# Modulation of a two-layer block gathered in one accumulator a layer, and the mixing steps in another order

## The reference

```python
c_act = jax.nn.silu(c)
for l in range(2):
    mod = c_act @ ada_w[l] + ada_b[l]        # 1024 -> 6144
    shift1, scale1, gate1, shift2, scale2, gate2 = split(mod, 6)
    h = rms_norm(x, norm1_g[l]) * (1 + scale1) + shift1
    z = h @ w_in[l]
    ...                                       # differential attention -> y_attn
    u = silu(layer_norm(causal_conv31(ga * sigmoid(gb)), conv_ln_g, conv_ln_b))
    y_conv = u @ w_conv_o[l]
    x = x + (1 + gate1) * ((g_attn * y_attn + g_conv * y_conv) @ w_out[l])
    h2 = rms_norm(x, norm2_g[l]) * (1 + scale2) + shift2
    f_gate, f_up = split(h2 @ w_ffn_in[l], 2)
    x = x + (1 + gate2) * ((silu(f_gate) * f_up) @ w_ffn_out[l])
out = rms_norm(x, final_g)
```

## Time and profile before

| | |
|---|---|
| median of the timed runs | 1102.91 us |
| the profiled execution's own time | 1105.96 us |
| its span | 1104.1 us |
| TensorE busy | 1079.3 us (98%) |
| VectorE busy | 821.9 us (74%) |
| ScalarE busy | 525.1 us (48%) |
| bytes read | 227 MB, mean 207 GB/s |
| VectorE, pieces | 84 of 1281 ns and 12 of 749 ns, 116.6 us |
| TensorE, group sums (L503) | 192 rows, 22.2 us |
| mean granted TensorE clock | 0.994 of full |

### The profile page before, as it was taken

How to read it: one execution, slowest core, us unless ns; L and a number is a source line. 1 busy time by engine, 2 the same in 40 slices (tenths; PEclk the granted TensorE clock), 3 DMA queues, 4 the chain that set the end, 5 groups by cost and what they waited for, 6 DMA issues and landing times.

```text
span 1104.1 us, 19435 instructions
## 1 busy us (share of the span) xinstructions
PE 1079.3 (98%) x8322; PEld 1028.9 (93%) x8322; DVE 821.9 (74%) x1096; ACT 525.1 (48%) x613; POOL 30.3 (3%) x54
## 2 busy tenths in 40 slices
PE   6999999999999999999999999999999999999998
PEld 5888799999998989979999999999898899999998
DVE  6878589887775899957887787869999576555552
ACT  4455665554434535545543433454455455344441
POOL 5100000000000010000000000000000000000000
PEclk9999999999999999999999999999999999999998
DMA  8666248888893554328698989846442375655551
GB/s 239 188 229 243 95 172 297 276 286 283 308 330 109 179 175 153 115 77 269 197 315 271 354 305 315 306 151 231 159 153 77 125 250 160 201 180 191 172 172 39
DMA packets 132845, 230.38 MB, mean 209 GB/s; under 512 B 6569, under 2 KB 60183, under 8 KB 132761
## 3 DMA queue, kind: packets, MB, share of 16 engines
q1 hardware_dynamic: 130404, 227.04, 61.3%
q0 software_dynamic: 1440, 0.85, 0.5%
q10 hardware_dynamic: 917, 1.27, 0.3%
HBM read 227.29 MB, written 1.06 MB: 207 GB/s over the span
## 4 chain that ended last, share of the span: by engine, by line
PE 71%; DVE 18%; ACT 6%; issue 3%; DMA 1%; SPq 0%; POOL 0%; DVEq 0%; POOLq 0%; ACTq 0%
PE mm L430 64%; DVE lo L1245 6%; DVE cacc L1335 5%; ACT hi L833 3%; PE mm L473 2%; PE pv L503 2%; ACT pB L912 1%; DVE ada_acc L1266 1%; DVE sB L1343 1%; DVE qk L1358 1%; PE pa L541 1%; DVE hf L1356 1%; DVE qk L1357 1%; DMA swap<-qk 1%; DMA xin<-in_x_dram 1%
## 5 line engine op out<-in xcount | busy, mean ns | idle before, releaser
L430 PE MATMUL mm<-act_hi,hi 128*128 128x256 f32 x1760 | 493.6, 284 | 2.5 <-ACT act_hi L901 1.8
L430 PE MATMUL mm<-act_hi,lo 128*128 128x256 f32 x1760 | 487.3, 280 | 0.0
L430 PE MATMUL mm<-act_lo,hi 128*128 128x256 f32 x1760 | 469.6, 280 | 0.0
L1245 DVE TENSOR_TENSOR lo<-raw,hi 128x2048 fp32r<-128x2048 f32 (+1 forms) x159 | 359.6, 2265 | 131.5 <-ACT hi L833 129.5
L833 ACT ACTIVATE hi<-raw 128x2048 fp32r<-128x2048 f32 (+1 forms) x160 | 302.1, 1892 | 232.0 <-PE mm L430 184.4
L430 PEld LDWEIGHTS mm<-act_hi,hi 128*128 128x128 f32 x1760 | 332.9, 189 | 6.4 <-issue 4.9
L430 PEld LDWEIGHTS mm<-act_hi,lo 128*128 128x128 f32 x1760 | 332.9, 189 | 0.4
L430 PEld LDWEIGHTS mm<-act_lo,hi 128*128 128x128 f32 x1760 | 322.2, 189 | 0.0
L430 PE MATMUL mm<-u_hi,hi 128*128 128x256 f32 x608 | 170.8, 281 | 0.0
L430 PE MATMUL mm<-u_lo,hi 128*128 128x256 f32 x608 | 169.8, 279 | 0.0
L430 PE MATMUL mm<-u_hi,lo 128*128 128x256 f32 x608 | 169.6, 279 | 0.0
(11 more groups left out here) (263 smaller groups left out, 950.3 us busy)
## 6 DMA issues: line engine op xcount, KB each, us to landing
ada_raw<-in_ada_w_dram SPq DMA_DIRECT2D x96, 512.0 KB, 5.7
raw<-in_w_ffn_in_dram SPq DMA_DIRECT2D x88, 512.0 KB, 5.4
raw<-in_w_in_dram SPq DMA_DIRECT2D x40, 1024.0 KB, 5.2
raw<-in_w_ffn_out_dram SPq DMA_DIRECT2D x20, 1024.0 KB, 6.2
raw<-in_w_up_dram SPq DMA_DIRECT2D x16, 1024.0 KB, 6.8
raw<-in_w_down_dram SPq DMA_DIRECT2D x16, 1024.0 KB, 7.7
raw<-in_w_out_dram SPq DMA_DIRECT2D x12, 1024.0 KB, 5.5
raw<-in_w_in_dram SPq DMA_DIRECT2D x16, 512.0 KB, 6.1
```

The costliest lines, as they stand in the source:

```text
L430: ins = pe.matmul(o, w[:, kk, fs], a[:, k, :], start=(k == 0 and i == 0 and f % 2 == 0), stop=(ends and i == len(pairs) - 1), skip_group_c ...
L1245: v(dve.tensor_tensor(lo[:, c % RING, 0:nk, :], raw[:, c % RING, 0:nk, :], hi[:, c % RING, 0:nk, :].bitcast(F32), ALU.subtract), "lo_done")
```

## The change

A piece is now 16 **contiguous rows** of `ada_w` (all 6144 columns, 384 KB). Partition 8k+b holds columns b\*768 to b\*768+767 of row k, 3072 bytes that lie together in memory. Each layer has 64 such pieces and one accumulator of 128 x 768, in a ring of four. silu(c) must then stand eight times over, each value on eight partitions: GpSimd spreads it (`c_wide`) and TensorE turns it. The sum over the 16 rows goes against an 8-column selector (`blocks`), so that one matmul gives eight column tiles: six matmuls a layer instead of 48. All of them stand at the norm ahead of the layer, none between chunks: layer 0's before the first block's last norm, layer 1's three within `sum_squares_late` and three behind it. VectorE adds the bias once a layer, ahead of `gain1`. Pieces: 10, 54 and 64 in the three stages. `keep_warm` has four matmuls more ahead of `up` and two more ahead of each FFN.

Beside that, in the mixing `heads_out(1, (1, 2))` comes ahead of the second sum, ScalarE's `heads_rstd(3)` and VectorE's `heads_normed(3)` come before the squares and their sum, and at the start lambda's matmul and its copy come one chunk earlier.

```diff
-ADA_W = D
-ADA_T = ADA_W // P
-ADA_GROUPS = MODS // ADA_T
-ADA_RING = 3
-ADA_ACCS = 2
-ADA_P = KD
+ADA_B = 8
+ADA_K = P // ADA_B
+ADA_T = MODS // ADA_B
+ADA_W = ADA_T * P
+ADA_RING = 4
+ADA_P = D // ADA_K
...
+    c[i, C_BLK + i % ADA_B] = 1.0
...
-    stages = [(range(first[("in", 2)] + 2, first[("out", 1)] + 1), 1, lambda c: 2.0 if c - first[("in", 2)] in (4, 6) else 1.0),
+    stages = [(range(first[("in", 2)] + 2, first[("out", 1)] + 1), 10, lambda c: 2.0 if c - first[("in", 2)] in (4, 6) else 1.0),
...
-                    src = t["ada_w_2"][i // ADA_GROUPS, k * P:(k + 1) * P, i % ADA_GROUPS * ADA_W:(i % ADA_GROUPS + 1) * ADA_W]
+                    src = t["ada_w_2"][l, k * ADA_K:(k + 1) * ADA_K, :].rearrange("k (b f) -> (k b) f", b=ADA_B)
...
-                if c in ada_at:
-                    ada_sums(c, ada_at)
...
+            def ada_sums(l, tiles):
+
+                if tiles[0] == 0:
+                    pe.wait_ge(sem("ada_used"), (l + 1) * ADA_P)
+                b = bank(2) if tiles[0] == 0 else pv[2]
+                for f in tiles:
+                    ins = pe.matmul(b[:, f:MODS:ADA_T], ada_acc[:, l, f * P:(f + 1) * P], blocks, start=(f == 0), stop=True, skip_group_check=True)
+                if tiles[-1] == ADA_T - 1:
+                    full(ins, 2)
...
+            wait("c_rows_ready")
+            full(pe.transpose(b[:, P + NMOD:P + NMOD + ADA_P], c_wide[0:ADA_P, :], ident[0:ADA_P, 0:ADA_P]), 0)
...
-            chunk(("in", 1), 1, act_hi, act_lo)
             wait("lam_ready")
             full(pe.matmul(bank(2)[:, 0:LAYERS], ones[0:1, :], lams[0:1, 8:8 + LAYERS], start=True, stop=True), 2)
+            chunk(("in", 1), 1, act_hi, act_lo)
...
-            ada_sums(first[("up", 0)], ada_between)
-            keep_warm(WARM + 0)
+            keep_warm(WARM + 4)
...
-                    ada_sums(first[(0, "in", 3)], ada_between)
+                    ada_sums(0, range(ADA_T))
...
-                heads_out(1, (1,))
+                heads_out(1, (1, 2))
                 sum_of("csq_added", hf[:, 0, :], 1)
-                heads_out(1, (2,))
...
-                ada_sums(first[(l, "ffn", 0)], ada_between)
-                keep_warm(2)
+                keep_warm()
...
-                    sum_squares_late()
-                    ada_sums(first[(1, "in", 3)], ada_between)
+                    sum_squares_late(between=lambda: ada_sums(1, range(0, ADA_T // 2)))
+                    ada_sums(1, range(ADA_T // 2, ADA_T))
                     keep_warm(2)
...
+                log_tables()
+                heads_rstd(3, full("a")[:, 0:S], "banka_free")
                 wait("centred")
                 a(act.activation(csq[:, :, :], cacc[:, :, :], ACT.Square), "csq_ready")
-                heads_rstd(3, full("a")[:, 0:S], "banka_free")
...
+            pool.dma_start(c_rows[0:ADA_P, :], t["c_2"][0].rearrange("(r p) -> r p", p=ADA_K)).then_inc(sem("c_rows_loaded"), 16)
...
+                ada_columns(l)
```

More of the change, by code:

```diff
@@ L68 @@
 C_ID, C_ONE = 0, P
-C_FREQ, C_ADD, C_UP = 2 * P, 2 * P + 1, 5 * P + 1
-C_ALL = 8 * P + 1
+C_FREQ, C_BLK = 2 * P, 2 * P + 1
+C_ADD = C_BLK + ADA_B
+C_UP = C_ADD + 3 * P
+C_ALL = C_UP + 3 * P
 def constants():
@@ L177, in two_blocks @@
     first = {name: ids[0] for name, (_, ids) in groups.items()}
[L178 to L185 removed]
+    pieces = LAYERS * ADA_P
+    stages = [(range(first[("in", 2)] + 2, first[("out", 1)] + 1), 10, lambda c: 2.0 if c - first[("in", 2)] in (4, 6) else 1.0),
+              (range(groups[("out", 0)][1][1], first[(0, "in", 3)]), ADA_P - 10, lambda c: 0.85 if c < first[("down", 0)] else 1.3),
+              (range(first[(0, "ffn", 0)], first[(1, "in", 3)]), ADA_P, lambda c: 1.0 if c < first[(0, "down", 0)] else 0.9)]
+    ada_pos = []
     for window, count, share in stages:
         until = np.cumsum([share(c) for c in window[:-2]])
[L188 to L192 removed]
+        for j in range(count):
+            ada_pos.append(window[int(np.searchsorted(until, (j + 0.5) / count * until[-1]))])
     pack, srcs = {}, [
         ("g_mix_pre", t["g_mix_pre"][0], KD), ("g_mlstm", t["g_mlstm_out"][0], MH), ("g_mix_post", t["g_mix_post"][0], KD),
[L199 removed]
+        ("g_mlp_pre", t["g_mlp_pre"][0], KD), ("g_mlp_post", t["g_mlp_post"][0], KD),
         ("final", t["final_g_2"], KD)]
@@ L246, in two_blocks @@
         ada_raw = sb("ada_raw", [P, ADA_RING, ADA_W])
[L247 removed]
+        ada_acc = sb("ada_acc", [P, LAYERS, ADA_W])
         cst = sb("cst", [P, C_ALL])
@@ L289, in two_blocks @@
         adab = sb("adab", [P, P], on=start)
+        c_rows = sb("c_rows", [P, ADA_K], on=start)
+        c_wide = sb("c_wide", [P, P], on=start)
         cwr = sb("cwr", [P, LAYERS, GF], on=start)
@@ L490, in chunk @@
                 ins.then_inc(sem("mm_done"), 1)
-                if c in ada_at:
-                    ada_sums(c, ada_at)
-            def ada_sums(c, where, part=None):
-                l, q, count = where[c]
-                for a in range(count) if part is None else (part,):
-                    i = l * ADA_GROUPS + q + a
-                    pe.wait_ge(sem("ada_used"), (i + 1) * ADA_P)
-                    b = bank(2) if a == 0 else pv[2]
-                    for f in range(ADA_T):
-                        to = a * ADA_T + f
-                        ins = pe.matmul(b[:, to:to + 1], ada_acc[:, i % ADA_ACCS, f * P:(f + 1) * P], ones[:, 0:1], start=(to == 0), stop=True,
-                                        skip_group_check=True)
-                    if a == count - 1:
-                        full(ins, 2)
+            def ada_sums(l, tiles):
[6 more added lines that the diff above has]
+                    full(ins, 2)
             def product(name, *acts, **kw):
@@ L534, in sums_of_added, with sum_squares_late @@
                 n("sq_ready", 2)
-            def sum_squares_late(last=((6,), (7,))):
+            def sum_squares_late(last=((6,), (7,)), between=None):
                 for tiles in ((4, 5),) + last:
+                    if between and tiles == last[0]:
+                        between()
                     wait("sq_ready")
@@ L601, in _ @@
             pe.transpose(b[:, 0:NROW], rows[0:NROW, :], ident[0:NROW, 0:NROW])
-            full(pe.transpose(b[:, P:P + NMOD], adab[0:NMOD, :], ident[0:NMOD, 0:NMOD]), 0)
+            pe.transpose(b[:, P:P + NMOD], adab[0:NMOD, :], ident[0:NMOD, 0:NMOD])
+            wait("c_rows_ready")
+            full(pe.transpose(b[:, P + NMOD:P + NMOD + ADA_P], c_wide[0:ADA_P, :], ident[0:ADA_P, 0:ADA_P]), 0)
             bank("a")
@@ L1457, in _ @@
             advance(groups[("in", 1)][1][0])
+            link(dve.tensor_copy(nlam[:], full(2)[:, 0:LAYERS]), "bank2_free")
             wait("tables_ready")
@@ L1460, in _ @@
             advance(groups[("in", 1)][1][1])
-            link(dve.tensor_copy(nlam[:], full(2)[:, 0:LAYERS]), "bank2_free")
             rope(qk1, swap1, 0, "k")
```

52 lines of the change are left out of this document (18 added, 34 removed).

## The result

The changed kernel takes 1095.68 us (median of 4 runs, 1094.22 to 1096.14), the kernel before 1103.13 (4 runs beside it): ratio 0.9927, 95% interval 0.9914 to 0.9939. It is faster by 7.45 us. The forecast was 1089.5 with a range of 1085.5 to 1095.0: right in sign, short of the size by half, and outside the range by 0.7.

The account below looks back on a forecast made before the run. TensorE, busy 98% of the span, was taken as the bound, with VectorE and ScalarE as slow in layer 0's FFN. Terms summed to 14.5 us off the profiled 1105.96, giving 1091.5; the median forecast was 1089.5, range 1085.5 to 1095.

Parts of the forecast that it names:

- Sums in block 1: First block: three sums between chunks, 1.68 us each on TensorE's path, go and nothing replaces them; 5.0 us won.
- A piece: VectorE's operation at 768 columns, estimated between rows of 256 and 1024 columns: 1.05 us start to start, bounds 0.99 and 1.315.
- Layer 0's FFN: With four pieces VectorE's and ScalarE's cycle, 11.94 us, exceeds TensorE's 11.3 and binds; 3.5 us won instead of 9.3.
- one of the prediction's own signs of being wrong: Anywhere in the profile after: the forecast is wrong if clock 0.50 shows at new places.
- The mixing: Second sum's wait falls from 1.95 to 0.1 us in each layer, 3.7, plus 1.7 of clock; 5.4 us won.
- The start: Lambda's matmul one chunk earlier: the 1.04 us wait for its copy goes, 0.25 comes; 0.8 us won.
- The norms: 0.15 us lost ahead of up, 0.2 won ahead of layer 1's FFN, 0.3 lost ahead of layer 1.
- From profile to median: Profile 3.05 us above median: 1088.4 if profiling's price, about 1090.1 if mostly low clocks; 1089.5 taken between.
- Rival 2: Waits in layer 0's FFN and ahead of layer 1 make the clock fall; two falls add 3.6 us, 1093.1; 22%.
- Rival 3: Mixing: the wait stays because the root or heads_normed(3) on VectorE delays the sum; 1093.2 us; 5%.
- Rivals 1: Layer 0's FFN: the cycle doesn't bind if a piece costs 0.89 us or less; 9.3 won, 1083.7 us; 12%.
- rival 4: Layer 0's FFN cycle: transfers of 3072-byte rows slow it; 32 us lost at 200 GB/s, 1121 us; 3%.

Follow-up runs that it names:

- before_placed: The kernel before with unused columns, so its activations start where the changed kernel's do within 256 bytes, no instruction altered; 1108.31 us, ratio 1.0052.
- after_again: The changed kernel run once more, nothing altered; 1093.86 us, ratio 0.992.
- mix_undone: The changed kernel with the old order of the mixing set back in its three places; 1096.26 us, ratio 0.9947.
- after: The changed kernel itself in its first profiled execution, against the kernel before; profiled 1095.38 us, median 1095.68 us, ratio 0.9927.
- u192: The changed kernel with 24 unused columns behind the lambdas, so u_hi and u_lo start at 192 of 256 bytes instead of 96; 1091.47 us, ratio 0.9892.
- share3: The changed kernel with eight more pieces in block 1 and three instead of four per group in layer 0's FFN; 1092.80 us, ratio 0.9908.
- share_b: The changed kernel with eight more pieces in block 1, 36 beside layer 0's FFN groups, 20 beside its down, never over two a chunk there; 1090.24 us, ratio 0.9881.

## Why the prediction was right, and where it was wrong

The sum was 14.5 us in the profile. First products of the stages (us from the span's start) give it by stage; `before_placed`, the changed kernel and `after_again` have equal places:

| first product of | before | before_placed | changed | after_again |
|---|---|---|---|---|
| `up` | 155.31 | 155.80 | 155.17 | 155.36 |
| layer 0 | 354.70 | 357.18 | 351.13 | 351.04 |
| layer 0's FFN | 531.45 | 532.38 | 524.31 | 525.06 |
| layer 1 | 732.94 | 734.16 | 723.83 | 724.12 |
| layer 1's FFN | 907.99 | 909.36 | 897.01 | 897.30 |
| end of the span | 1104.1 | 1106.0 | 1093.3 | 1088.9 |

- **Sums in block 1** (5.0 forecast). At equal places 5.4 to 5.7 (201.38 against 195.96 and 195.68). Right. Against the bare kernel before only 3.4, since the rows went slower.
- **A piece** (1.05 from start to start). 1.015 and 1.05: right. The Trainium skill's table (VectorE: DVE Perf Modes, "The TRN2 errata"), which gave 0.86, is not what the trace shows.
- **Layer 0's FFN** (3.5 forecast). The mechanism was right to the hundredth: 11.94 us, TensorE waiting for `lo` for 4.6 us (some 4 forecast). From product 0 to 10 the trace has 661.14 - 539.56 = 121.6, of which 120.5 were forecast; the rest, 1.1, is one cycle of 13.06 that waited for a transfer, where I charged 0.8 in all. The stage gave 2.3 (201.78 to 199.52) and 2.7. The term was mis-sized by some 1 us: the transfer, the slower u rows (0.1183) and in the first trace a clock that fell in a new place, which was one of the prediction's own signs of being wrong.
- **The mixing** (5.4 forecast). 2.3 measured, the largest miss of a term. The second sum's wait fell to 0.17 as forecast (0.1). Two steps failed. "What follows finds its first input at about 486.0" left out that the convolution needs a bank as well, which VectorE frees 0.4 after TensorE comes; 1.15 a layer instead of 1.85. And the 1.7 us of clock were no part of the change: the same wait of 1.95 had a fall in layer 0 before, in layer 1 in `mix_undone`, and none in `before_placed`.
- **The start** (0.8). 0 to 0.6: the wait for lambda's copy went, but TensorE waits 0.54 or 0.97 us for lambda's matmul where 0.25 was charged. **The norms** came out as forecast (0.25 lost ahead of layer 1).
- **From profile to median.** Of the 3.05 us the forecast took 2.0 off (1091.5 to 1089.5), in part as a price of profiling. No run shows such a price. Single runs of the kernel before spread from 1098.7 to 1105.9 in later comparisons, and its first profiled execution was at the top; the profile of the changed kernel was within 0.3 of its median.
- **Rivals 2 and 3** (1093.1, the clock falls elsewhere, and 1093.2, the mixing's wait stays) came nearest in number. Rival 2 doesn't explain the miss: `after_again` has no fall ahead of the end of the span and `after` has one, at 584, for 1.7 us. Rival 3's mechanism did not come, since the second sum waits 0.17, though the mixing did win less. Rivals 1 and 4 fell: the cycle binds, and transfers cost 1.1 us in one cycle. (In rival 4 the bound "about 215 GB/s" should be some 227, 1.57 MB in 13.0 - 6.1 us; nothing rests on it.)

**Which steps failed.** The miss of 6.2 us (1095.68 against 1089.5) adds up from the profile: the profiled execution came 3.9 later than forecast (1095.38 against 1091.5), 2.0 were taken off on the way from profile to median, and 0.3 lie between the two after. The 3.9 by stage, before less changed, with the forecast in brackets: ahead of `up` 0.1 (0.65), block 1 3.4 (5.0), layer 0 up to its FFN 3.6 (3.55), its FFN 2.0 (3.2), layer 1 up to its FFN 1.9 (1.85), the rest -0.2 (0.2).

So in that pair of traces the mixing looks right, and this is luck. The order gave 1.15 a layer. The other 3 us were in the main a clock that happened to fall in the trace of the kernel before (1.7), and rows of `in` that happened to go at 0.1133 in the changed kernel's (0.84 a layer: 173.18, where `after_again` in layer 0 and `u192` in layer 1 take 174.0). The mixing's term failed all the same: 5.4 was charged and 2.3 is what the order gives.

The other step is one that the prediction did not write down: "TensorE needs 96 x 0.117 = 11.3 us" was carried over as if a row's duration belonged to its form. It belongs to its form and its place, and the change moves the places. In the profiled pair that cost 2 us of block 1's 5.4; by the medians of the kernel before in both places, 5.2 us in all.

The measured terms (5.5 + 2.5 + 2.3 + 0.4) give some 10.7 at equal places and paces. The timed 12.6 and 13.2 have 2 to 3 more, about as much as their intervals allow. They come near the 13.4 that was forecast against the median of 1102.91, but not because the terms were right. That the changed kernel has 0.1133 more often than the one before at the same place would give the rest: six traces of it with `act_hi` at distance 64 have 512 to 2144 rows so, counted by 16 without a stall (`after`, `after_again`, `mix_undone`, `share3`, `share_b`, `u192`), and `before_placed` has 128. But that is one trace for the kernel before, and why it should be so stays open.

## What to carry to other kernels

Before you take a matmul's duration over to a changed kernel, ask whether the change resizes or moves an allocation: rows of one form ran from 0.1133 to 0.12 us by the distance of the moving operand from the weights within 256 bytes, and some 200 unused bytes a partition were worth about as much as the whole change. So compare two versions at equal places, then choose the place by itself; here a few unused columns gave 11 to 13 us and moving eight pieces to where VectorE had room gave 4 to 5. Where a wait goes, list everything that the next instruction needs, its bank too.
